# One GpSimd instruction instead of two for the low part of a weight unit in a decoder trunk kernel

## What is computed

```python
for l in range(DEPTH):
    h = rms_norm(x, mix_norm_g[l])
    p_gdn, p_mla, p_rwkv, p_dsa, p_gate = _split(h @ w_in[l], SLAB_SPLITS)
    y_a = gdn_mixer(p_gdn, ...) @ w_out_gdn[l]
    ...
    merged = g_a * y_a + g_b * y_b + g_c * y_c + g_d * y_d
    x = x + merged @ w_o[l]
    hm = rms_norm(x, mlp_norm_g[l])
    x = x + jnp.square(jax.nn.relu(hm @ w_up[l])) @ w_down[l]
return rms_norm(x, final_norm_g)
```

## Time and profile before

| | us |
|---|---|
| median of 3 runs | 2008.43 |
| lowest, highest | 2008.21, 2009.43 |
| the profiled execution | 2010.22 |
| span from its first to its last instruction | 2008.4 |

### The profile page before, as it was taken

One profiled execution on the slowest core, in us unless ns is written; L12 is line 12 of the kernel. 1 busy time (PEld: TensorE's weight loads), 2 busy tenths in 40 slices (PEclk: granted clock), 3 DMA queues, 4 the chain that ended last, 5 costly groups with the idle time before them and its releaser, 6 DMA issues.

```text
span 2008.4 us, 32189 instructions
## 1 busy us (share of the span) xinstructions
PE 1957.3 (97%) x13220; PEld 1550.1 (77%) x13220; DVE 1100.3 (55%) x1827; ACT 794.9 (40%) x1304; POOL 794.7 (40%) x617
## 2 busy tenths in 40 slices
PE   7999999999999999999999999999999999999997
PEld 6788887766677888888877878777676788888886
DVE  8786756888743322222487666389886342222223
ACT  6443613345353432332354354234545444332323
POOL 3432513433334444444444133244332444444442
PEclk9999999999999999999999999999999999999999
DMA  6220212321322333233332111123122233323322
GB/s 236 84 70 29 64 44 63 97 61 43 126 74 78 119 96 95 95 100 99 95 126 84 40 41 61 54 75 94 53 86 82 74 94 95 95 95 96 104 95 74
DMA packets 52066, 170.05 MB, mean 85 GB/s; under 512 B 5824, under 2 KB 14144, under 8 KB 51280
## 3 DMA queue, kind: packets, MB, share of 16 engines
q1 hardware_dynamic: 50928, 163.97, 25.5%
q0 software_dynamic: 992, 4.02, 0.6%
HBM read 160.88 MB, written 7.08 MB: 84 GB/s over the span
## 4 chain that ended last, share of the span: by engine, by line
PE 84%; DVE 11%; ACT 2%; issue 1%; DMA 0%; POOL 0%; ACTq 0%; SPq 0%; DVEq 0%
PE bank_a L513 12%; PE bank_a L514 12%; PE bank_a L519 12%; PE bank_v L519 7%; PE bank_v L513 7%; PE bank_v L514 7%; PE bank_v L671 3%; DVE arena L2061 1%; DVE arena L1576 1%; DVE m L2059 1%; PE bank_a L821 1%; PE bank_f L604 1%; DVE mg L1582 1%; PE bank_v L590 1%; DVE mg L1751 1%
## 5 line engine op out<-in xcount | busy, mean ns | idle before, releaser
L478 POOL TENSOR_TENSOR w_lo<-ring,w_hi 128x512 fp32r<-128x512 f32 x536 | 733.2, 1389 | 879.2 <-ACT w_hi L1225 870.3
L513 PE MATMUL bank_a<-h_hi,w_hi 128*128 128x512 f32 x1296 | 518.0, 400 | 0.0
L514 PE MATMUL bank_a<-h_lo,w_hi 128*128 128x512 f32 x1296 | 505.2, 390 | 0.0
L1225 ACT ACTIVATE w_hi<-ring 128x1024 fp32r<-128x1024 f32 x268 | 281.6, 1051 | 222.9 <-DVE arena L2194 212.4
L519 PE MATMUL bank_a<-h_hi,w_lo 128*128 128x512 f32 x1296 | 320.4, 389 | 0.0
L513 PEld LDWEIGHTS bank_a<-h_hi,w_hi 128*128 128x128 f32 x1296 | 243.2, 188 | 67.6 <-issue 16.7
L514 PEld LDWEIGHTS bank_a<-h_lo,w_hi 128*128 128x128 f32 x1296 | 243.4, 188 | 54.6 <-issue 5.3
L519 PEld LDWEIGHTS bank_a<-h_hi,w_lo 128*128 128x128 f32 x1296 | 243.1, 188 | 50.5
L513 PE MATMUL bank_v<-parts,w_hi 128*128 128x512 f32 x640 | 250.5, 391 | 2.7 <-DVE parts L2163 2.7
L514 PE MATMUL bank_v<-parts,w_hi 128*128 128x512 f32 x640 | 249.1, 389 | 0.0
L1576 DVE TENSOR_TENSOR sg<-bank_v,sg 128x512 f32<-128x512 f32 x112 | 77.4, 691 | 295.9 <-PE bank_v L519 239.4
(11 more groups left out here) (305 smaller groups left out, 2710.8 us busy)
## 6 DMA issues: line engine op xcount, KB each, us to landing
ring<-in_w SPq DMA_DIRECT2D x268, 512.0 KB, 3.5
out_ring<-in_w SPq DMA_DIRECT2D x64, 128.0 KB, 3.5
x_dram<-arena SPq DMA_DIRECT2D x2, 2048.0 KB, 9.0
arena<-x_dram SPq DMA_DIRECT2D x2, 2048.0 KB, 9.2
arena<-in_x SPq DMA_DIRECT2D x2, 1024.0 KB, 9.0
out_x<-arena SPq DMA_DIRECT2D x4, 512.0 KB, 4.0
consts<-in_const SPq DMA_DIRECT2D x1, 1253.0 KB, 13.3
arena<-tabs POOLq DMA_DIRECT2D x2, 512.0 KB, 3.9
```

The source lines that it names most:

```text
L478: ins = nc.gpsimd.tensor_tensor(w_lo[:, g % SPLIT, ks, :], raw, w_hi[:, g % SPLIT, ks, :].bitcast(F32), ALU.subtract)
L513: mm(b[:], w_hi[:, s, k, :], hi[:, k, :], start=k == 0, stop=False)
L514: mm(b[:], w_hi[:, s, k, :], lo[:, k, :], start=False, stop=False)
L1225: act_fn(w_hi[:, g % SPLIT, :, :], ring[:, g % RING, :, :], ACT.Copy).then_inc(S["split_hi"], 1)
```

## The change

The loop over two halves of four tiles goes, and one subtraction takes all eight tiles. The wait ahead of it and the count behind it are the same.

```diff
                 pool.wait_ge(S["split_hi"], g + 1)
                 if u == RAW_UNITS + 1:
                     pool.wait_ge(S["n_h"], at(l, "n_h", 2 * KT))
-                for half in range(2):
-                    ks = slice(4 * half, 4 * half + 4)
-                    raw = ring[:, g % RING, ks, :]
-                    ins = nc.gpsimd.tensor_tensor(w_lo[:, g % SPLIT, ks, :], raw, w_hi[:, g % SPLIT, ks, :].bitcast(F32), ALU.subtract)
+                ins = nc.gpsimd.tensor_tensor(w_lo[:, g % SPLIT, :, :], ring[:, g % RING, :, :], w_hi[:, g % SPLIT, :, :].bitcast(F32), ALU.subtract)
                 ins.then_inc(S["split_lo"], 1)
```

## The result

The changed kernel takes 2023.74 us (median of three runs, 2023.07 to 2028.04) against 2008.43 (2008.21 to 2009.43): a ratio of 1.0081, 95% interval 1.0063 to 1.0099 (ratios and intervals are estimated from all runs of both kernels, so they differ a little from the quotient of the two medians, here 1.0076). The forecast was 2021.3, in a range from 2012 to 2027, with slower at 0.82. The profiled execution took 2023.74 us for a span of 2021.9.

A forecast was written before the change was run, and what follows sets the result against it. PE bounds the kernel, waiting mainly for DVE, which GpSimd's subtractions lock out. Delays of 6.6 us a layer, 13.2 in both, less 0.3 give +12.9: from 2008.43 to 2021.3 us, range 2012 to 2027.

The forecast's parts named there:

- 1, near 456: First attention's start: L1790 ends at 457.37 instead of 456.28 with PE already waiting for it, +1.09 us a layer.
- 2, near 180: Recurrence: L1582 ends at 180.25 instead of 179.16 and delays L1724, which PE's next step needs, +0.83 us a layer.
- 3, near 537: Second attention's start: a held L1751 moves L1790's end to 537.49 from 536.84, PE waiting, +0.65 us a layer.
- 4, near 614: Ahead of `wo`: held L1751 moves the next L1751's end to 613.97 from 613.12, PE waiting, +0.85 us a layer.
- 5, near 551: Inside the second attention: L1790 ends 1.09 us later, less 0.27 us of slack at PE, +0.82 us a layer.
- 5, near 466: Same pattern as near 551, a delayed L1790, with 0.59 us of slack at PE: +0.50 us a layer.
- 6, near 662: MLP's start: L1591 ends at 662.11 instead of 661.01, with 0.61 us of slack at PE, +0.49 us a layer.
- 7, all: Mostly convolutions: nine pairs of GpSimd halves meeting two L1582, in busy DVE stretches, 9 x 0.16 = +1.4 us a layer.
- The start: Each layer's first unit, where PE waits for `split_lo`: the shorter GpSimd work gains 0.15 us, 0.3 for both layers.
- that DVE gets in anyway: Rival: GpSimd gives way inside its instruction, terms 1 to 7 vanish, 2004.8 us; no change by either way 0.16.
- that the delay is absorbed: Rival: PE has other work, half of places 1, 3 and 4 remains, 2010.7 us; no change by either way 0.16.
- the one on the slower side: Rival: ten more GpSimd-DVE meetings a layer become visible to PE at half size, +11, 2032 us; chance 0.06.

The follow-up runs named there:

- e1: Kernel before the change, with one long subtraction in only two units of each layer, halves elsewhere: 2016.54 us in one run, against 2009.47.
- e11: The changed kernel run once more beside the kernel before the change: 2025.63 us against 2008.99, ratio 1.0079.
- e2: Kernel before the change, its two subtractions per unit split over 2 and 6 tiles instead of two halves: 2013.81 us against 2009.47, ratio 1.0023.
- e3: Kernel before the change, with four subtractions of two tiles per unit instead of two halves: 2004.57 us against 2009.47, ratio 0.9975.
- e4: Changed kernel, with GpSimd waiting in 8 units of each layer until DVE has passed what PE needs: 2005.99 us against 2009.47 before the change, ratio 0.9983.
- e10: Changed kernel with ten such GpSimd waits per layer, one instruction over all eight tiles: 1999.97 us against 2008.99 before the change, ratio 0.9955.

## Why the prediction was right

It was right by its own mechanism. The delay of PE's instructions against before, by how much it grows within a microsecond or two at each place, read from their starts in the two traces:

| Place | Predicted, us | Layer 1 | Layer 2 |
|---|---|---|---|
| 1, near 456 | 1.09 | 1.09 | 1.08 |
| 2, near 180 | 0.83 | 0.81 | 0.81 |
| 3, near 537 | 0.65 | 0.60 | 0.61 |
| 4, near 614 | 0.85 | 0.85 | 0.86 |
| 5, near 551 | 0.82 | 0.76 | 0.78 |
| 5, near 466 | 0.50 | 0.50 | 0.47 |
| 6, near 662 | 0.49 | 0.56 | 0.56 |
| 7, all | 1.4 | 1.54 | 1.60 |
| sum | 6.6 | 6.7 | 6.8 |

What lies outside these places was not foreseen and nearly cancels: +0.2 us up to 27 us, +0.4 near 160, -0.1 near 540, -0.1 at L871 of the second layer (foreseen as -0.15), -0.55 from 1140 to 1149, -0.24 near 1267, +0.25 near 1528, +0.3 near 1999, together +0.15.

- **GpSimd's price**: 2.38 us assumed, 2.396 measured. The estimate from the Trainium skill's figure (GPSIMD Engine Reference, section 3.1), 2.25 us, was 0.15 too low; the line through two lengths of the same trace was the better source.
- **GpSimd's busy time** was to fall by some 40 us and fell by 76.7 on this line. The sum of before held 54 us in which halves waited for DVE; the long ones waited for 268 x 0.054 = 14 us (mean 2450 ns against a median of 2396). The 268 x 0.15 = 40 us left out that fall, another 40 us. It costs nothing, since GpSimd isn't waited for.
- **Places 1 to 6** came within 0.1 us each, the slack guesses of 5 and 6 included.
- **Place 7** came near in its sum, but partly by another way than the nine equal pairs, so that its nearness is in part luck: the five pairs from 93 to 119 us and what follows on them show up as one step of 0.85 us at 131, of which 0.5 is the double meeting at 119.98 (from the start of the first of the two to DVE's next work on a bank 6.93 us, before 6.43). The pairs near 52, 208, 479 and 524 gave 0.13, 0.21, 0.14 and 0.21 where 0.16 each was said.
- **The start**: 0.13 us of the foreseen 0.15 at L871 of the second layer. At the first layer's start a second L1625 was held and PE waited 0.65 us for it, which was not foreseen; that stretch as a whole (from 10 to 27 us) came out 0.4 us shorter all the same, in a part where executions of one kernel differ by as much.
- **The term that was missing**: the sum says +12.9, the profiled spans differ by 13.5, the medians by 15.3 and, with more runs, by 16.6. What is over comes at least in part from the clock. A wait of PE that grew from 1.3 to 2.2 or 2.4 us is now in some executions followed by a stretch at half clock, each worth 1.1 to 1.6 us (e1 twice, e11 twice, the first trace of the changed kernel never: 4 of the 12 waits of this length in the three). Of the first three runs of the changed kernel the slowest, 2028.04 us, has the lowest mean clock, 0.991, and the fastest, 2023.07 us, the highest, 0.994. In the trace of before only the two waits of 3 us near 537 and 1524 had that (and the program's two ends). The prediction priced each added microsecond of waiting at one microsecond.
- **Rivals**: that DVE gets in anyway fell with L1748's 2.44 us; that the delay is absorbed fell with PE's waits for DVE, which grew by 12.5 us in all; the one on the slower side was wrong too, no ten further meetings a layer became visible.

## What to carry to other kernels

Where GpSimd and DVE read SBUF side by side, the price of a GpSimd instruction is not its length but which DVE instruction starts inside it, and who waits for that one. Find that place by laying the two engines' rows beside each other; here holding GpSimd back by one semaphore wait in ten units of a layer (11.4 us gained with halves, 9.0 with one long instruction) was worth more than the best size (4.9 us gained with quarters; one piece lost 16.6). Merging instructions saves a fixed part on an engine with time to spare and takes away the seams through which another engine gets in.

## What the runs showed of the hardware

- The GpSimd subtraction took 1288 ns for 128x512 and 2396 for 128x1024; a memset of 128x1024 took 955 ns, a TENSOR_SCALAR with one input 2772 ns, longer than with two inputs.
- The Trainium skill (SBUF — State Buffer, "Who interferes with whom") has the pair of ports held "for the whole instruction". For the subtraction every row here agrees, at 256, 512 and 1024 columns. GpSimd's TENSOR_SCALAR let a two-input DVE instruction in 1.04 us after its start, 1.73 us before its end, and kept out L1787, which came 2.10 us after its start, to its end, so for that form the measurement says otherwise.
- The granted clock fell to half behind some waits of PE of 2.2 to 2.4 us and not behind others of the same length in the same program; at the second attention's start it fell with all 12 waits of 2.6 to 3.7 us (before, after, e1, e2, e3, e11) and with 11 of the 14 of 1.8 to 2.4 us (e4 to e10), for 3.4 or 6.8 us.
- A seam doesn't always let DVE in: at 15.33 us of the trace of before, an L1628 that reached the exclusion together with a pair of halves took 3.06 us in place of 0.75, kept out by both.
